# Key products of 32 expert tiles in plain fp32 during key search and gate making; gate table keyed outermost

## The reference, cut to what matters

```
q = (xn @ w_query).reshape(bsz, seq, PEER_HEADS, 2, PEER_HALF)
s = jnp.einsum('bthsc,hsnc->bthsn', q, sub_keys)
top_s, top_i = lax.top_k(s, PEER_TOPK)            # 16 of 128 keys, twice, for 8 heads
cand_s = top_s[..., 0, :, None] + top_s[..., 1, None, :]
best_s, best_pos = lax.top_k(cand_s, PEER_TOPK)   # 16 pairs of keys: 16 experts a head
expert_idx = take(top_i[0] * 128 + top_i[1], best_pos)
gate = jax.nn.softmax(best_s, axis=-1)
u = jnp.take(expert_u, ib, axis=0)
act = gb * jax.nn.gelu(jnp.einsum('pkd,pd->pk', u, xb))
vv = jnp.take(expert_v, ib, axis=0)
y = jnp.einsum('pk,pkd->pd', act, vv)
```

## Time and profile before

| | |
|---|---|
| Median of 3 runs | 3950.51 us (3942.04 to 3961.04) |
| Profiled execution | 3944.23 us, its span 3942.4 us |
| Mean granted clock of TensorE | 0.951 |
| TensorE matmuls busy | 3484.3 us, 88% of the span |
| VectorE busy | 2259.6 us, 57% |
| ScalarE busy | 1538.7 us, 39% |
| GpSimd busy | 271.3 us, 7% |
| Key search, from VectorE's last query scores on | 1055 to 1119 us in the first layer |
| Gate making | 1119 to 1231 us |
| Experts | 1231 to 1955 us |

### The profile page before, as it was taken

The page is one execution under the profiler, slowest core; times in us unless marked ns, Lnnn a source line. Parts: engine busy times, 40 slices in busy tenths (PEclk is TensorE's granted clock), DMA queues, the critical chain, the costliest instruction groups (busy, mean ns, idle before and its releaser), DMA issues. The chain is left out here.

```text
span 3942.4 us, 65111 instructions
## 1 busy us (share of the span) xinstructions
PE 3484.3 (88%) x21036; PEld 3059.2 (78%) x21036; DVE 2259.6 (57%) x4715; ACT 1538.7 (39%) x2901; POOL 271.3 (7%) x201
## 2 busy tenths in 40 slices
PE   7999978988748999999889999799885589999997
PEld 6777767876647999999777777678775479999996
DVE  3544435652697666666534445356427976666665
ACT  2322323321146555555432223242211565555554
POOL 1101000110021000000011011001000200000000
PEclk9999989989879999999999999899897899999999
DMA  3212211312103555555322212122130035555553
GB/s 113 82 59 73 87 42 67 107 64 93 52 5 107 186 187 186 187 186 187 136 99 69 88 44 87 50 82 94 54 142 2 5 130 186 187 187 188 186 187 117
DMA packets 121908, 432.76 MB, mean 110 GB/s; under 512 B 15713, under 2 KB 18017, under 8 KB 120929
## 3 DMA queue, kind: packets, MB, share of 16 engines
q1 hardware_dynamic: 121824, 431.74, 31.4%
HBM read 430.64 MB, written 1.05 MB: 109 GB/s over the span
## 5 line engine op out<-in xcount | busy, mean ns | idle before, releaser
L236 PE MATMUL bank<-arena,ring 128*128 128x256 f32 x4160 | 996.7, 386 | 44.2 <-PEq L188 12.8
L1871 DVE TENSOR_TENSOR tile_parts<-raw_tiles,tile_parts 128x512 fp32r<-128x512 f32 x1024 | 708.8, 693 | 504.2 <-ACT tile_parts L1831 504.0
L1831 ACT ACTIVATE tile_parts<-raw_tiles 128x512 fp32r<-128x512 f32 x1024 | 646.6, 632 | 641.3 <-PE bank L1772 632.5
L236 PEld LDWEIGHTS bank<-arena,ring 128*128 128x128 f32 x4160 | 771.6, 194 | 143.7 <-issue 45.0
L1770 PE MATMUL bank<-xhigh,tile_parts 128*128 128x256 f32 x2048 | 578.8, 283 | 1.1 <-DVE tile_parts L1871 1.0
L1772 PE MATMUL bank<-xhigh,tile_parts 128*128 128x256 f32 x2048 | 579.6, 283 | 0.0
L1771 PE MATMUL bank<-xlow,tile_parts 128*128 128x256 f32 x2048 | 579.5, 283 | 0.0
L1770 PE MATMUL bank<-tile_parts,act_high 128*128 128x512 f32 x1024 | 402.0, 393 | 1.6 <-DVE tile_parts L1871 1.6
L1770 PEld LDWEIGHTS bank<-xhigh,tile_parts 128*128 128x128 f32 x2048 | 392.1, 191 | 12.3 <-DVE tile_parts L1871 2.5
L1771 PE MATMUL bank<-tile_parts,act_high 128*128 128x512 f32 x1024 | 401.5, 392 | 0.0
L1771 PEld LDWEIGHTS bank<-xlow,tile_parts 128*128 128x128 f32 x2048 | 392.1, 191 | 9.7
(11 more groups left out here) (317 smaller groups left out, 4417.7 us busy)
## 6 DMA issues: line engine op xcount, KB each, us to landing
raw_tiles<-in_u SPq DMA_DIRECT2D x256, 512.0 KB, 3.4
raw_tiles<-in_v SPq DMA_DIRECT2D x256, 512.0 KB, 3.5
ring<-in_w_side SPq DMA_DIRECT2D x80, 512.0 KB, 3.5
ring<-in_w_gdn SPq DMA_DIRECT2D x64, 512.0 KB, 3.5
ring<-in_w_rwkv SPq DMA_DIRECT2D x48, 512.0 KB, 6.2
ring<-in_w_gdn_side SPq DMA_DIRECT2D x32, 512.0 KB, 3.5
ring<-in_p_gdn SPq DMA_DIRECT2D x16, 512.0 KB, 4.3
ring<-in_w_out SPq DMA_DIRECT2D x16, 512.0 KB, 3.4
```

The costliest lines, as they stand in the source:

```text
L236: mm = te.matmul(ps, ring[:, slot, k * P:(k + 1) * P], x[:, k, :], start=(k == 0), stop=(k == KT - 1))
L1831: a.activation(f32r(hi[:, cols]), raw[u % 2][:, cols], ACT.Copy).then_inc(high_done, 1)
L1871: v.tensor_tensor(f32r(lo[:, cols]), raw[u % 2][:, cols], hi[:, cols], ALU.subtract).then_inc(low_done, 1)
```

## The change

1. *Early tiles.* The last 16 tiles (`EARLY`, keys 112 to 127) have their key products made in the key search block, in plain fp32 (8 matmuls of 256 columns): four before the first transposes and twelve after. Their raw tiles use the ring of the query tiles. ScalarE's Gelu writes them into `GATES`, where the gate will be multiplied in.
2. *Kept tiles.* The first 16 tiles (`KEPT`) have theirs made in gate making, in plain fp32, two matmuls in each group; Gelu writes them to `kept`.
3. *Gate table keyed outermost* (`p (j t)`): a tile's gates are contiguous, ScalarE's copy writes runs of four. TensorE writes its product of a token to every fourth element of the bank. ScalarE copies 112 of the keys, VectorE multiplies the other 16 into the early activations.
4. *One-hots by four tokens.* Columns are now a comparison on VectorE over four tokens and a multiplication with the gate on GpSimd. All is done per group, in turns of eight groups.
5. *Experts* in three runs: 16 kept tiles and 16 early ones with value products alone, then 96 with both. The value parts have two buffers, the key parts one. The input is split between the kept and the early tiles instead of in key search.
6. *Memory laid out by hand*: `kept` lies where the raw key tiles come later, the input's low part where the plain input lay, and so on; the norm writes to `xf` there.

The core of the diff, cut:

```diff
+    GATES = arena[:, :].rearrange("p (j t) -> p j t", t=T)
+    EARLY, KEPT, EARLY_FIRST = 16, 16, 4
+    FIRST_EARLY = NK - EARLY
...
+        eq = left.rearrange("p s k -> p (s k)").rearrange("p (x a) -> p x a", a=TOPK)
...
-                v.tensor_tensor(f32r(xlow[:]), xn, xhigh[:], ALU.subtract).then_inc(x_low, 1)
...
+                for m in range(EARLY):
+                    if m < 8:
+                        sp.wait_ge(EQ.sem, EQ.at(f"q{m}", 1))
+                    else:
+                        sp.wait_ge(EU.sem, EU.at(f"u{m - 8}"))
+                    sp.dma_start(ring[:, m % 8], A["u"][l, FIRST_EARLY + m]).then_inc(early_in[m % 8], 16)
...
+                weights_out(0)
+                for m in range(EARLY):
+                    hidden_out(m)
+                    if m == EARLY_FIRST - 1:
+                        slots_out(0)
+                    if m == EARLY - 4:
+                        weights_out(1)
+                slots_out(1)
...
+                for i in range(NB):
+                    for m in (range(EARLY_FIRST), range(EARLY_FIRST, EARLY))[i]:
+                        early(m)
```

Gate making, by engine:

```diff
+                def one_hots(i, r):
+                    if r % 2 == 0:
+                        v.wait_ge(made, FIRST + 8 * i + r - 3)
+                        v.tensor_tensor(rows(r), keys, of_tokens(slot1, i, r), ALU.is_equal).then_inc(rows_vec, 1)
+                    v.wait_ge(made, FIRST + 8 * i + r - 1)
+                    v.tensor_tensor(cols(r), keys, of_tokens(slot2, i, r), ALU.is_equal).then_inc(cols_vec, 1)
+
+                def group(i, r):
+                    v.wait_ge(moved, FIRST + 8 * i + r + 1)
+                    act = GATES[:, FIRST_EARLY:, tokens(i, r)]
+                    v.tensor_tensor(act, act, by_key(r)[:, FIRST_EARLY:], ALU.mult).then_inc(scaled, 1)
+                    if not last(i, r, 2):
+                        one_hots(i, r + 2)
...
+                def group(i, r):
+                    if r % 2:
+                        g.wait_ge(made, FIRST + 8 * i + r - 3)
+                        g.tensor_tensor(rows(r), keys, of_tokens(slot1, i, r), ALU.subtract).then_inc(rows_pool, 1)
+                    g.wait_ge(cols_vec, FIRST + 8 * i + r + 1)
+                    g.tensor_tensor(cols(r), cols(r), of_tokens(slotg, i, r), ALU.mult).then_inc(cols_pool, 1)
...
+                def group(i, r):
+                    te.wait_ge(cols_pool, FIRST + 8 * i + r + 1)
+                    te.wait_ge(*((rows_act, FIRST + 4 * i + r // 2 + 1) if r % 2 else (rows_vec, FIRST + 4 * i + r // 2 + 1)))
+                    te.wait_ge(scaled, FIRST + 8 * i + r - 3)
+                    for u in range(4):
+                        mm = te.matmul(by_key(r)[:, :, u], rows(r)[:, u], cols(r)[:, u], start=True, stop=True)
+                    mm.then_inc(made, 1)
...
+                    for k in range(2 * (r % 4), 2 * (r % 4) + 2):
+                        mm = te.matmul(banks[4 + n][:, 0:T], u_ring[:, n, k * P:(k + 1) * P], xf[:, k], start=(k == 0), stop=(k == KT - 1))
...
+                def one_hots(i, r):
+                    a_.wait_ge(rows_pool, FIRST + 4 * i + r // 2 + 1)
+                    a_.activation(rows(r), rows(r), ACT.Abs).then_inc(rows_abs, 1)
+                    a_.wait_ge(rows_abs, FIRST + 4 * i + r // 2 + 1)
+                    a_.activation(rows(r), rows(r), ACT.Relu, scale=-1.0, bias=ones[:, 0:1]).then_inc(rows_act, 1)
+
+                def group(i, r):
+                    if r % 2 and not last(i, r, 2):
+                        one_hots(i, r + 2)
+                    a_.wait_ge(made, FIRST + 8 * i + r + 1)
+                    a_.activation(GATES[:, 0:FIRST_EARLY, tokens(i, r)], by_key(r)[:, 0:FIRST_EARLY], ACT.Copy).then_inc(moved, 1)
+                    if r % 4 == 3:
+                        n = r // 4
+                        a_.wait_ge(tile_done, FIRST + 2 * i + n + 1)
+                        a_.activation(kept[:, bass.ds(2 * i + n, 1)], banks[4 + n][:, 0:T].unsqueeze(1), ACT.Gelu_apprx_tanh).then_inc(tile_out, 1)
```

Experts:

```diff
+                def value(kind, a, r):
+                    sp.wait_ge(v_low, FIRST + 2 * (base[kind] + a + r) - 2)
+                    v_tile(sp, l, column[kind] + a + r, r % 2)
...
+                def kept_step(a, r):
+
+                    v.wait_ge(a_low, FIRST + a + r - 1)
+                    v.tensor_tensor(act[r % 2].unsqueeze(1), kept[:, of(a, r)], GATES[:, of(a, r)], ALU.mult).then_inc(gated, 1)
+                    low_act("kept", a, r)
+                    low_v("kept", a, r)
...
+                def new_step(a, r):
+                    if not ends(a, r, 2):
+                        with_u(a, r + 2)
+                    with_v("new", a, r)
...
+                groups_of(a_, NA // UJ, UJ, UJ, kept_step)
+                a_.activation(f32r(xhigh[:, :]), xf[:, :], ACT.Copy).then_inc(x_high, 1)
+                groups_of(a_, NE // UJ, UJ, UJ, early_step)
+                groups_of(a_, NU // UJ, UJ, UJ, new_step)
...
+                groups_of(v, NA // UJ, UJ, UJ, kept_step)
+                v.wait_ge(x_high, 1)
+                v.tensor_tensor(f32r(xlow[:, :]), xf[:, :], xhigh[:, :], ALU.subtract).then_inc(x_low, 1)
```

More of the change, by code:

```diff
@@ L1575, in _ @@
                     SQ.end()
[L1576 to L1582, removed]
+                weights_out(0)
[6 more added lines that the diff above has]
+                slots_out(1)
                 a.wait_ge(S.sem, S.now())
+                a.wait_ge(SU.sem, SU.now())
             @block.tensor
@@ L1615, in _ @@
                         te.transpose(banks[4 + n][:, 0:P], flat(src[i]), ident).then_inc(E.sem, E.one(f"t{n}_{i}"))
[L1617 to L1627, removed]
-    def peer_gate_phase(l):
[L1635 to L1644, removed]
+    def peer_gate_phase(l):
+        NG = T // 4
+        FIRST = 4
+        rows_vec, rows_pool, rows_act, cols_vec, cols_pool, made, moved, scaled, tile_done, tile_out = [lsem("gt_" + n) for n in (
+            "rows_vec", "rows_pool", "rows_act", "cols_vec", "cols_pool", "made", "moved", "scaled", "tile_done", "tile_out")]
+        rows_abs = lsem("gt_rows_abs")
+        oh1, oh2 = onehot[:, 0:16], onehot[:, 16:24]
+        rows = lambda r: oh1[:, 4 * (r % 4):4 * (r % 4) + 4]
+        cols = lambda r: oh2[:, 4 * (r % 2):4 * (r % 2) + 4]
+        last = lambda i, r, ahead: isinstance(i, int) and 8 * i + r + ahead >= NG
+        keys = iota.unsqueeze(1).to_broadcast([P, 4, NK])
+        of_tokens = lambda x, i, r: x[:, bass.ds(32 * i + 4 * r, 4)].unsqueeze(2).to_broadcast([P, 4, NK])
+        tokens = lambda i, r: bass.ds(32 * i + 4 * r, 4)
+        by_key = lambda r: banks[r % 4][:, :].rearrange("p (k u) -> p k u", u=4)
         with nc.Block() as block:
@@ L1664, in _ @@
+                one_hots(0, 1)
+                groups_of(v, NG // 8, 1, 8, group)
+                v.wait_ge(scaled, FIRST + NG)
             @block.gpsimd
             def _(g):
-                G.prime(g)
-                with g.Fori(0, NI) as i:
-                    G.begin()
-                    for x in range(2):
-                        g.wait_ge(E.sem, E.before(f"g{2 * x + 1}", i))
-                        against_slot1(g, i, 2 * x + 1, ALU.subtract).then_inc(G.sem, G.one(f"rows{x}"))
-                    G.end()
+                def group(i, r):
[4 more added lines that the diff above has]
+                    g.tensor_tensor(cols(r), cols(r), of_tokens(slotg, i, r), ALU.mult).then_inc(cols_pool, 1)
@@ L1674, in _ @@
+                for x in (rows_pool, cols_pool):
+                    g.sem_inc(x, FIRST)
+                g.wait_ge(made, FIRST)
+                groups_of(g, NG // 8, 1, 8, group)
             @block.tensor
             def _(te):
-                E.prime(te)
-                with te.Fori(0, NI) as i:
-                    E.begin()
-                    for g in range(4):
-                        te.wait_ge(S.sem, S.before(f"g{g}", i))
-                        for u in range(4 * g, 4 * g + 4):
-                            te.wait_ge(V.sem, V.at(f"u{u}", i))
-                            if u % 8 == 4:
-                                te.wait_ge(S.sem, S.at(f"rows{u // 8}", i))
-                            mm = te.matmul(banks[g][:, (u % 4) * NK:(u % 4 + 1) * NK], oh1[:, u], oh2[:, u % 8], start=True, stop=True)
-                        mm.then_inc(E.sem, E.one(f"g{g}"))
-                    E.end()
```

375 lines of the change are left out of this document (217 added, 158 removed).

## The result

After the change the median is 4027.57 us (4026.19 to 4035.97, 4 runs) against 3947.32 us for the kernel before (3942.04 to 3961.04, 4 runs): a ratio of 1.0202, interval 1.0172 to 1.0233. It is 80 us slower; 88 on a base of 3950.5 had been forecast. The profiled execution took 4026.2 us against 3944.2.

What follows compares the result with a forecast made beforehand. VectorE bounds key search and gate making, TensorE the experts; after the change a loop of waits paces gate making. Per layer 1 + 128 - 85 = +44, twice +88 on 3944.2: 4032, median 4038 us; forecast 4005 to 4075, range 3965 to 4115.

Steps and rivals of the forecast that it cites:

- the ring over two groups: Gate making: queue orders of ScalarE, GpSimd and VectorE close a loop of waits, 7.35 us for two groups, stage 240 us.
- the exclusion: Gate making: VectorE and GpSimd operations with two SBUF inputs run one after the other, adding 1.04 us to the cycle.
- break-even of 6.0 us a turn: Gate making: a cycle under 6.0 us for two groups (growth of 84) would make the change faster.
- TensorE's share: Gate making: TensorE's work per group, at most 1.1 us for one-hot products plus 0.96 for two kept-key matmuls, 2.06 us.
- Experts: -85 us: Expert stage, per layer: 92.2 us of key products saved, less 1 for value-tile pace, 3 for rounding, 3 for opening.
- The 3 us at the border: Expert stage: rounding the input between kept and early tiles makes TensorE lose 3 us.
- Exclusion costs little: Rival, gate making: loop stays but loses 1.04, cycle 6.31 us, stage 207, whole 3972 us; chance 0.13.
- Dearer operations: Rival, gate making: multiplications 1.27 us and strided copies 0.9, together 34 us a layer, whole 4106 us; chance 0.17.
- Gate making is TensorE's: Rival: ScalarE never waits for rows, cycle 4.1 us, stage 136 us, whole 3830 us; chance 0.09.
- Slowed one-hot products: Rival, gate making: PSUM writes four columns apart slow the matmuls; at factor 4, stage 348, whole 4254 us; chance 0.04.
- Table loads: Rival, gate making: Abs after Gelu needs table reloads, 41 us a layer, whole 4120 us; chance 0.02.
- the signs named beforehand: Profile after: gate making 235 to 250 us, GpSimd busiest, comparisons stretched, ScalarE idle before Abs, experts near 639, key search unchanged.

Runs made afterwards that it cites:

- e1: The changed kernel without the key products of the 16 kept tiles in gate making (output not the reference's): 4029.09 us, ratio 1.0206.
- e3: The changed kernel with GpSimd's row subtraction for odd group r + 2 placed before its multiplication for group r + 1: 3897.65 us, ratio 0.9872.
- e5: The changed kernel with ScalarE copying an odd group before, not behind, making the rows of the group two on: 3960.19 us, ratio 1.0042.
- e4: The changed kernel with columns made token by token on VectorE with two scalars, and no multiplication on GpSimd: 3822.75 us, ratio 0.9687.
- e2: The changed kernel with the key numbers for VectorE's comparisons taken from a PSUM bank instead of SBUF: 3986.14 us, ratio 1.0102.
- e7: The changed kernel with the edits of e2 and e4 together: 3793.15 us, ratio 0.9615.
- e9: e7 with the first two early value tiles asked for ahead of the wait and of the two key tiles: 3794.69 us, ratio 0.9619.

## Why the prediction was right

**Key search: +1 us, measured 0.** The products fit with room, since a tile took less than the 3.83 us put down: ScalarE's Gelus of the early tiles follow one another every 3.45 us. The last transposes wait for VectorE, as assumed (TensorE idle 5.01 us from 1109 on).

```profile
1105.51 0.39 ACT L1599 ACTIVATE arena<-bank 128x256 f32<-128x256 f32 x1 [3.07 <-PE bank L1662]
1108.96 0.39 ACT L1599 ACTIVATE arena<-bank 128x256 f32<-128x256 f32 x1 [3.07 <-PE bank L1662]
...
1114.04 0.47 PE L1672 MATMUL bank<-made_of_shapes,arena 128*128 128x128 f32 x1 [5.01 <-DVE arena L1576]
```

**Gate making: +128 us, measured +123.6 and +121.8.** The step that carried the forecast, the ring over two groups, is shown from both sides: it stands in the profile row by row; leaving out a third of TensorE's instructions changes nothing (e1), and cutting the ring in one queue (e3), another (e5) or by its GpSimd work (e4) takes 66, 35 and 103 us off. The turn was 7.23 us, not 7.35. Of its terms the exclusion cost 0.85 in place of 1.04, and GpSimd began 0.17 us after VectorE's end (1203.62 to 1203.79), not 0.07. The half Gelu, 0.18, isn't on the ring. From the odd copy's start to VectorE's rows it is 1.55 and 1.61 us (1199.94 to 1201.49, and again a turn later), where the prediction's terms for this stretch add up to 0.49 + 0.94 = 1.43. Errors of both signs cancel in part here, and the sum came closer than its terms. The first and last ends took 1 to 3 us rather than 4.8. The break-even of 6.0 us a turn also stands: e2 at 6.6 and e5 at 6.2 are slower than before by 1.0 and 0.4%, e3 at 5.2 (each stage over 32) is faster by 1.3%.

TensorE's share was put too high: 2.06 us a group, where e7 has 1.76. Its "at most 1.1" for 8 records doesn't follow from 12 in 1.85 us, which would give 1.23; they cost 0.89 from start to start, and the two kept-key products 0.87 in place of 0.96 (1199.73, 1200.62 and 1201.49 in e4's timeline). In the changed kernel this costs nothing, as TensorE isn't the bound.

**Experts: -85 us, measured -81.8 and -79.9.** The mechanism is right; two terms were too small. Value-only tiles go at 2.79 us in the kept half, as forecast (2.78), but at 2.91 in the early half: 1.7 us (first layer). The first step with key products in it again takes 6.84 where 5.62 would do: 1.2 us. The 3 us at the border were right in size (3.5), but by luck: the rounding of the input, priced at 3, is 1.7 by itself (e9), and what ended last was the values asked for behind two key tiles, which the prediction didn't have. The 96 full tiles take 5.62 us each.

**The rivals.** *Exclusion costs little*: e2 is this case made real, 3986 us where 3972 was worked out. *Dearer operations*: neither came; the multiplication's own work is 1.04 us and the strided copy 0.53. *Gate making is TensorE's*: not in this kernel, and not in e4 either; in e7 TensorE and VectorE are both full. *Slowed one-hot products*: none; the Trainium skill, Advanced Engine Details and Errata, section Memory Cachelines, would have them slow, and e4's rows don't show it for a stride of four fp32 columns. *Table loads*: none in the whole stage; between Gelu (1207.58), copy and the next Abs, in this timeline of ScalarE that goes on from the one above:

```profile
1213.15 0.63 ACT L1756 ACTIVATE onehot<-onehot 128x512 f32<-128x512 f32 x1 [4.76 <-POOL onehot L1719]
```

**The sum.** +88 us was forecast for the profiled execution and +82.0 measured: 10.6 us less for gate making and 2 for key search, 8.3 more for the experts, and 1 less for the unchanged rest. The other 5 us of the miss of 10 are in the step to the median: I set it 6.3 us above the profiled execution, as it was before, and it lay 1.4 above. Of the signs named beforehand, GpSimd as the busiest engine of gate making didn't come: TensorE is busy 155.0 us there and GpSimd 110.5. The others came or were near.

## What to carry to other kernels

When work is dealt out over engines, adding up each engine's share gives only a floor: here the floor was put at 4.1 us for two groups (3.5 as e7 has it), and the ring of waits made it 7.2. Follow one buffer through the queues until you are back at it, and sum what stands in each queue ahead of the next link; where the sum is above the busiest engine's, look for one instruction that can stand elsewhere in its queue, before the work is changed. An instruction moved by one place in GpSimd's queue was worth 66 us a layer; and a wait that doesn't shorten when its cause is removed may have a second cause that ends at almost the same time.

## What the runs showed of the hardware

- GpSimd and VectorE exclude each other also when VectorE runs a comparison with two scalars and one tensor from SBUF: four take 1.91 us beside GpSimd's subtraction, 1.10 alone. With the tensor in PSUM they take 1.36 us, beside it or not (e4, e7).
- ScalarE's copy into runs of four fp32 values, 1 KB apart, costs no more than a contiguous one (448 elements in 0.53 us), while VectorE's read of single values with a stride had cost half more (0.62 us against 0.43).
- In gate making, where TensorE waits for other engines, its mean granted clock was 0.84 after the change (busy 155 of 236 us) and 0.61 in e1 (123 of 233 us), a mean over stretches at 2.4 and at 1.2 GHz; e1's stage is no longer for it. In e3 it was 0.98, with 123 of 167 us busy. Seen alone, a low clock is no evidence that TensorE is the bound.
